# A hybrid decoder layer on one core: weight blocks with their k-tiles woven column by column

## What is computed

```python
xn = rmsnorm(x, mix_norm_g)
p = xn @ w_in                       # one projection, 1024 -> 10,256 columns
ya, yb, yc, yd = mlstm(...), short_conv_mixer(...), mamba2_mixer(...), stick_breaking_attention(...)
lifted = einsum('bsie,ied->bsid', stack([ya, yb, yc, yd]), w_lift)
merged = einsum('bsid,bsid->bsd', sigmoid(gates), lifted)
x = x + merged @ w_out
x = x + conv_glu_mlp(rmsnorm(x, ffn_norm_g), w_up, ffn_conv_w, ffn_conv_b, w_down)   # D_FF = 2816
return rmsnorm(x, final_norm_g)
```

## Time and profile before

| | |
|---|---|
| median of the runs | 1038.17 us (2 runs, 1037.79 to 1038.56) |
| the profiled execution | 1038.42 us |
| its span, first to last instruction | 1036.7 us |
| busy PE | 1019.0 us, 98% |
| busy PEld | 837.8 us, 81% |
| busy DVE | 593.2 us, 57% |
| busy ACT | 424.3 us, 41% |
| DMA | 108.24 MB, mean 104 GB/s |
| mean granted TensorE clock | 0.992 of full speed (2.4 GHz) |

### The profile page before, as it was taken

How to read it: one execution, slowest core, us unless ns; L and a number is a source line. 1 busy time by engine, 2 the same in 40 slices (tenths; PEclk the granted TensorE clock), 3 DMA queues, 4 the chain that set the end, 5 groups by cost and what they waited for, 6 DMA issues and landing times.

```text
span 1036.7 us, 12635 instructions
## 1 busy us (share of the span) xinstructions
PE 1019.0 (98%) x4724; PEld 837.8 (81%) x4724; DVE 593.2 (57%) x764; ACT 424.3 (41%) x515; POOL 67.6 (7%) x74
## 2 busy tenths in 40 slices
PE   8999999999999999999999999989999999999996
PEld 7897888887777887777888888868888888888886
DVE  6835754656676566556364456687656666543323
ACT  5514445644435322444432333544444344332331
POOL 5610000000000000000000000320000000000002
PEclk9999999999999999999999999989999999999998
DMA  6332222223222333343252222513233222253312
GB/s 238 114 113 70 82 84 82 77 93 105 89 85 82 120 122 124 132 132 103 81 183 87 97 88 97 181 61 119 85 100 101 100 86 88 68 176 94 102 56 81
DMA packets 32024, 108.24 MB, mean 104 GB/s; under 512 B 3684, under 2 KB 5860, under 8 KB 31600
## 3 DMA queue, kind: packets, MB, share of 16 engines
q1 hardware_dynamic: 29520, 93.86, 27.1%
q0 software_dynamic: 2320, 13.69, 4.0%
q10 hardware_dynamic: 144, 0.14, 0.1%
HBM read 103.42 MB, written 4.25 MB: 104 GB/s over the span
## 4 chain that ended last, share of the span: by engine, by line
PE 93%; DVE 4%; ACT 2%; issue 1%; DMA 1%; DVEq 0%; SPq 0%; ACTq 0%
PE gb L413 81%; PE gb L446 4%; DVE w_lo L985 1%; PE xb L596 1%; PE gb L524 1%; PE xb L556 1%; PE xb L549 1%; PE xb L536 1%; PE xb L413 1%; ACT w_hi L701 1%; PE xb L513 1%; DMA raw<-w_stream 1%; DVE y_lo L993 1%; PE gb L464 1%; PE xb L584 0%
## 5 line engine op out<-in xcount | busy, mean ns | idle before, releaser
L985 DVE TENSOR_TENSOR w_lo<-raw,w_hi 128x1024 fp32r<-128x1024 f32 (+2 forms) x181 | 218.1, 1206 | 342.8 <-ACT w_hi L701 342.4
L701 ACT ACTIVATE w_hi<-raw 128x1024 fp32r<-128x1024 f32 (+2 forms) x181 | 183.8, 1017 | 413.5 <-PE gb L413 380.8
L413 PE MATMUL gb<-xn_hi,w_hi 128*128 128x512 f32 x720 | 285.0, 396 | 0.0
L413 PE MATMUL gb<-xn_hi,w_lo 128*128 128x512 f32 x720 | 281.1, 390 | 0.0
L413 PE MATMUL gb<-xn_lo,w_hi 128*128 128x512 f32 x720 | 281.0, 390 | 0.0
L413 PE MATMUL gb<-y_hi,w_hi 128*128 128x512 f32 x400 | 159.1, 398 | 6.0 <-DVE y_lo L993 4.2
L413 PEld LDWEIGHTS gb<-xn_hi,w_hi 128*128 128x128 f32 x720 | 135.8, 189 | 29.7 <-issue 1.0
L413 PEld LDWEIGHTS gb<-xn_lo,w_hi 128*128 128x128 f32 x720 | 135.8, 189 | 29.0 <-issue 1.4
L413 PEld LDWEIGHTS gb<-xn_hi,w_lo 128*128 128x128 f32 x720 | 135.6, 188 | 28.6
L413 PE MATMUL gb<-y_lo,w_hi 128*128 128x512 f32 x400 | 156.6, 391 | 0.0
L413 PE MATMUL gb<-y_hi,w_lo 128*128 128x512 f32 x400 | 156.4, 391 | 0.0
(11 more groups left out here) (231 smaller groups left out, 1018.4 us busy)
## 6 DMA issues: line engine op xcount, KB each, us to landing
raw<-w_stream SPq DMA_DIRECT2D x149, 512.0 KB, 3.3
raw<-w_down SPq DMA_DIRECT2D x16, 384.0 KB, 3.0
abc<-scr_a POOLq DMA_DIRECT2D x8, 640.0 KB, 4.1
raw<-w_down SPq DMA_DIRECT2D x16, 320.0 KB, 2.8
x_in<-xT SPq DMA_DIRECT2D x8, 256.0 KB, 6.5
x<-xT POOLq DMA_DIRECT2D x1, 2048.0 KB, 8.5
scr_x<-x POOLq DMA_DIRECT2D x1, 2048.0 KB, 7.4
x<-scr_x POOLq DMA_DIRECT2D x1, 2048.0 KB, 8.4
```

The costliest lines, as they stand in the source:

```text
L413: ins = pe.matmul(out, w[:, r, lo:hi], rhs(k)[x], start=(first and n == 0 and q == 0), stop=(last_ and n == len(ks) - 1 and q == 2))
L701: act.activation(w_hi[:, r, 0:n], raw[:, r, 0:n], ACT.Copy).then_inc(S["hi_ready"], 1)
L985: dve.tensor_tensor(w_lo[:, r, 0:n], raw[:, r, 0:n], w_hi[:, r, 0:n].bitcast(F32), ALU.subtract)\
```

## The change

The host weaves the k-tiles of a block column by column: column c of k-tile n now lies at c * 8 + n, so one k-tile's columns are 8 fp32 elements, 32 bytes, apart. In the down-projection the blocks have 6 or 5 k-tiles, and the step is 24 or 20 bytes. In a lift block the two outputs' four k-tiles each are woven as eight. On the chip only the weight operand of `gemm` and of the small block changes: it reads with that step instead of contiguously. The blocks with tokens on the partitions keep `slabs`. DMAs, splits, waits and the order of all instructions stay the same.

```diff
@@ -61,6 +61,7 @@
 DOWN_K0 = [0, 6, 12, 17]
 N_UNITS = U_DOWN + 4 * KD
 RING = 4
+LANES = 8
 
 GL = {U_GL_D: 0, U_GL_A: 1, U_GL_B: 0, U_GL_C: 1}
 
@@ -405,12 +406,16 @@
 
     @block.tensor
     def _(pe):
-        def gemm(out, r, c0, rhs, ks, kk0=0, kstep=1, first=True, last_=True):
+        def ktile(w, r, kk, lanes=LANES, n=P):
+
+            c0 = kk // lanes * lanes * P + kk % lanes
+            return w[:, r, c0:c0 + lanes * (n - 1) + 1:lanes]
+
+        def gemm(out, r, kk, rhs, ks, first=True, last_=True, lanes=LANES):
 
             for n, k in enumerate(ks):
-                lo, hi = c0 + n * P, c0 + n * P + P
                 for q, (w, x) in enumerate(((w_hi, 0), (w_hi, 1), (w_lo, 0))):
-                    ins = pe.matmul(out, w[:, r, lo:hi], rhs(k)[x], start=(first and n == 0 and q == 0),
+                    ins = pe.matmul(out, ktile(w, r, kk + n, lanes), rhs(k)[x], start=(first and n == 0 and q == 0),
                                     stop=(last_ and n == len(ks) - 1 and q == 2))
             return ins
 
@@ -457,11 +462,11 @@
                 def yk(k):
                     return y_hi[s][:, k, :], y_lo[s][:, k, :]
                 for q in range(2):
-                    ins = gemm(gb(o + q)[:, :], u % RING, q * T, yk, range(4))
+                    ins = gemm(gb(o + q)[:, :], u % RING, 4 * q, yk, range(4))
             elif u == U_SMALL:
                 for k in range(KD):
                     for q, (w, x) in enumerate(((w_hi, 0), (w_hi, 1), (w_lo, 0))):
-                        ins = pe.matmul(gb(o)[0:96, :], w[:, u % RING, P * k:P * k + 96], xn(k)[x],
+                        ins = pe.matmul(gb(o)[0:96, :], ktile(w, u % RING, k, n=96), xn(k)[x],
                                         start=(k == 0 and q == 0), stop=(k == KD - 1 and q == 2))
             else:
                 ins = gemm(gb(o)[:, :], u % RING, 0, xg if u < U_DV else xn, range(KD))
@@ -477,7 +482,7 @@
             for u in (0, 1):
                 if k == 0:
                     pe.wait_ge(S["lo_ready"], u + 1)
-                ins = gemm(GB[u][:, :], u, k * P, xg, [k], first=(k == 0), last_=(k == KD - 1))
+                ins = gemm(GB[u][:, :], u, k, xg, [k], first=(k == 0), last_=(k == KD - 1))
         ins.then_inc(S["unit_done"], 2)
 
         for u in range(U_OUT):
@@ -608,7 +613,7 @@
             for k in range(KD):
                 if u == U_OUT:
                     pe.wait_ge(S["merged_ready"], k + 1)
-                ins = gemm(gb(first_tile[u])[:, :], u % RING, k * P, mg, [k], first=(k == 0), last_=(k == KD - 1))
+                ins = gemm(gb(first_tile[u])[:, :], u % RING, k, mg, [k], first=(k == 0), last_=(k == KD - 1))
             ins.then_inc(S["unit_done"], 1)
 
 
@@ -648,7 +653,7 @@
                 if t == 0:
                     pe.wait_ge(S["f_lo"], DOWN_K0[q] + DOWN_K[q])
                 gemm(GB[DOWN_BANK[t]][:, :], (U_DOWN + q) % RING, 0, hk, range(DOWN_K0[q], DOWN_K0[q] + DOWN_K[q]),
-                     first=(q == 0), last_=(q == 3)).then_inc(S["unit_done"], 1)
+                     first=(q == 0), last_=(q == 3), lanes=DOWN_K[q]).then_inc(S["unit_done"], 1)
         with pe.Fori(0, KD // 2 - 1) as i:
             for t in range(2):
                 down(i, t)
@@ -669,7 +674,8 @@
                 if e == 0 and q == 0:
                     pe.wait_ge(S["psum_read_dve"], DOWN_READ + KD - 2)
                 ins = gemm(O_LAST[e][:, 0:TH], (U_DOWN + q) % RING, 0, hk_half,
-                           range(DOWN_K0[q], DOWN_K0[q] + DOWN_K[q]), first=(q == 0), last_=(q == 3))
+                           range(DOWN_K0[q], DOWN_K0[q] + DOWN_K[q]), first=(q == 0), last_=(q == 3),
+                           lanes=DOWN_K[q])
                 if e == 1 and q == 0:
                     last_sum(0)
             ins.then_inc(S["o_last"], 1)
...
@@ -1412,9 +1418,15 @@
     (aq, ak, av, ao, ai, af, bb, bc, bx, cz, cx, cdt, sq, sk, sv, gt) = [w_in[:, c[n]:c[n + 1]] for n in range(16)]
     stream = np.zeros((N_STREAM, P, 1024), np.float32)
 
+    def lanes(w, n=LANES):
+
+        k, c = w.shape
+        w = w.reshape(k // (P * n), n, P, c).transpose(2, 0, 3, 1)
+        return np.ascontiguousarray(w).reshape(P, -1)
+
     def put(u, w, width=P):
         for n in range(w.shape[1] // width):
-            stream[u + n] = slabs(w[:, n * width:(n + 1) * width])
+            stream[u + n] = lanes(w[:, n * width:(n + 1) * width])
 
     def put_tokens(u, w):
         for n in range(2):
@@ -1424,30 +1436,31 @@
     put(U_DQ, sq); put(U_DK, sk); put_tokens(U_DV, sv)
     small = np.zeros((D, P), np.float32)
     small[:, 0:4], small[:, 32:36], small[:, 64:72] = ai, af, cdt
-    stream[U_SMALL] = slabs(small)
+    stream[U_SMALL] = lanes(small)
     put(U_AQ, aq); put(U_AK, ak); put_tokens(U_AV, av); put(U_AO, ao)
     put(U_Z, cz); put(U_XBC, cx)
     for n in range(4):
         for q, w in enumerate((bc, bx, bb)):
-            stream[U_B + 3 * n + q] = slabs(w[:, n * P:n * P + P])
+            stream[U_B + 3 * n + q] = lanes(w[:, n * P:n * P + P])
     lift = f["w_lift"][0]
     for u0, b in ((U_GL_D, 3), (U_GL_A, 0), (U_GL_B, 1), (U_GL_C, 2)):
         for t in range(4):
             for q in range(2):
                 d0 = P * (2 * t + q)
-                stream[u0 + 3 * t + q] = slabs(gt[:, D * b + d0:D * b + d0 + P])
-                stream[u0 + 3 * t + 2, :, 512 * q:512 * q + 512] = slabs(lift[b][:, d0:d0 + P])
+                stream[u0 + 3 * t + q] = lanes(gt[:, D * b + d0:D * b + d0 + P])
+            both = [lift[b][:, P * n:P * n + P] for n in (2 * t, 2 * t + 1)]
+            stream[u0 + 3 * t + 2] = lanes(np.concatenate(both))
     put(U_OUT, f["w_out"][0])
     up = f["w_up"][0]
     for t in range(NFF):
         for q in range(2):
-            stream[U_UP + 2 * t + q] = slabs(up[:, FF * q + P * t:FF * q + P * t + P])
+            stream[U_UP + 2 * t + q] = lanes(up[:, FF * q + P * t:FF * q + P * t + P])
     down = np.zeros((4 * KD, P, 6 * P), np.float32)
     wd = f["w_down"][0]
     for t in range(KD):
         for q in range(4):
             k0, n = DOWN_K0[q], DOWN_K[q]
-            down[4 * t + q, :, 0:n * P] = slabs(wd[k0 * P:(k0 + n) * P, t * P:t * P + P])
+            down[4 * t + q, :, 0:n * P] = lanes(wd[k0 * P:(k0 + n) * P, t * P:t * P + P], n)
 
     def cols(v):
```

More of the change, by code:

```diff
@@ L624, in _ @@
                         pe.matmul(X[0][:, :], ones[:], f_ac[:], start=True, stop=True).then_inc(S["n2_sum"], 1)
-                ins = gemm(gb(first_tile[u])[:, :], u % RING, k * P, x1g, [k], first=(k == 0), last_=(k == KD - 1))
+                ins = gemm(gb(first_tile[u])[:, :], u % RING, k, x1g, [k], first=(k == 0), last_=(k == KD - 1))
             ins.then_inc(S["unit_done"], 1)
@@ L635, in _ @@
                         pe.wait_ge(S["n2_ready"], k + 1)
-                    ins = gemm(GB[(TILES0 + BANK0 + q) % 4][:, :], (U_UP + q) % RING, k * P, mg, [k], first=(k == 0),
+                    ins = gemm(GB[(TILES0 + BANK0 + q) % 4][:, :], (U_UP + q) % RING, k, mg, [k], first=(k == 0),
                                last_=(k == KD - 1))
```

## The result

The woven kernel takes 1113.84 us (2 runs, 1112.41 to 1115.26) against 1038.17 us: 7.3% slower, ratio 1.0729 with a 95% interval of 1.0667 to 1.079. I had forecast 1054 us with a range up to 1077. The span of the profiled execution grew from 1036.7 to 1110.7 us, by 74.0 us.

A forecast was written before the change was run, and what follows sets the result against it. It took TensorE's matmuls, their number times a pace, to bound the kernel. 1038.4 us plus 0, 12.9 (last tile) and 3.1 (uncovered loads) gave 1054.4, stated as 1054, range 1036 to 1077 us.

The forecast's parts named there:

- The frame: Whole kernel: time is a number of matmuls times a pace; layout, split and DMA cost nothing, token blocks stay unchanged.
- Step one: 3822 matmuls of 512 columns in `gemm`: loads at 218 ns stay under the 227 ns pace, cost 0.
- the doubled reading: Strided weight loads of 128 columns read for 213 ns, twice as long, at 1.67 ns per new 16-byte piece.
- a fixed swap: Every `gemm` matmul: 13.3 ns on top of columns / 2.4, the same at 512 and 256 columns.
- A cover of 115 ns: 512-column matmuls: pace of 227 ns against 112 for loads alone hides longer loads; 9 ns left after the change.
- The prediction's last sentence: Signs of being wrong: step's price over 1.73 ns per column, or starts over 227 ns apart with short loads.
- Step two: Last tile, 132 matmuls of 256 columns: 218 ns replaces 120, 98 ns each, 12.9 us.
- Step three: Loads no fast matmul covers, after waits and the mixers' fp32 matmuls: 29 x 107 ns, 3.1 us.
- The free step: Rival, 31%: strided loads lose nothing and stay at 188 ns; time 1038 us, at most 1040.
- the heavy bound: Rival, 17%: each load element waits for the store, TensorE paces at 325 or 432 ns; 1448 or 1872 us.
- The load just exceeds its cover: Rival, 9%: the 13.3 ns swap follows the load, pace 232 ns in both streams; 1075 us.
- its threshold of 1.73: Load price in ns per column, (227 - 5) / 128, deciding that rival; only 0.06 above the proven rate.

The follow-up runs named there:

- first streams: Only fp32r matmuls with weight loads, no decoder layer, twelve load steps by matmul width; 512 columns: 226.7 ns at 4 bytes, 243.8 at 32.
- second streams: Matmul-and-load-only kernels, real moving operand against one repeated column; 512 columns, 32-byte load: 244.8 against 237.8 ns; contiguous load: 226.7 against 215.8.
- the streams: Kernels without the decoder layer: rows of 33 fp32r matmuls with loads of one step, nothing beside them; only start-to-start distance counts.
- the timed kernels: Against the kernel before: only the last projection woven, 1055.84 us (18.5 us more); only that projection's last tile woven, 1051.3 us (14.3 us more).

## Why the prediction was wrong

**The frame held.** The kernel is a number of matmuls times a pace; no layout, split or DMA cost anything, and the token blocks kept their loads. The size is explained by the paces: 3360 matmuls of 512 columns at 32 bytes, 17.1 ns each by the first streams (243.8 less 226.7), 57.5 us by that for 57.4 measured; and the last projection, 462 x 11 ns and 132 x 107.5 ns, 19.3 us for 18.5 measured. The second streams have 244.8 ns, which would give 60.8 us, so the streams price the kernel to some 3 us.

**Step one failed.** It read "218 is under 227 ... Cost 0" and cost about 62 us, 57.4 in the blocks before the last projection and 4 to 5 in seven tiles of it (18.5 less 14.3 by the timed kernels, 5.0 by the traces). Two terms in it were wrong, and they are different in kind:

- *The price of the load.* I took the doubled reading, 218 ns, from the fastest rate of new pieces that the contiguous moving operand shows. At 64 bytes the load alone takes 217 ns and at 20 and 24 about 222, so a doubling is near the truth for these steps; at this kernel's 32 bytes it is 238 ns, above the cover of 227 by itself. The inference from one operand's rate to the other's had no basis: a moving operand at 32 bytes takes a new piece every 0.84 ns where the load needs 1.86 (237.8 / 128). I read a rate that was merely used as if it were the limit.
- *The cover.* I took 226.7 ns as the matmul's own property, 213.3 and a fixed swap, "there is no loss to relieve". The clash streams show 215.8 ns without the moving operand's reads. The reads of the load and those of the matmul beside it get in each other's way (in which part of the chip isn't shown), and a load whose reads are scattered does so more: 6.4 ns per matmul at 8 bytes, with the load fully covered. A cover of 115 ns says when the load ends, not what it costs the work that covers it.

Of the 18.1 ns in the second streams (244.8 less 226.7), 11.1 are there by the load alone (237.8 less 226.7) and 7.0 by the clash on top (244.8 less 237.8). The prediction's last sentence names just these two as the signs of being wrong, a price over 1.73 ns per column and a moving stream slowed by a strided load, yet the second had no term in the sum and no chance of its own.

**Step two held, a little low.** 12.9 us foretold for the last tile, 14.3 measured: 226 ns from start to start where I had 218. In the streams the load alone takes 221 to 222 ns at these steps, and 227 to 228 under the real moving operand of 256 columns.

**Step three held for each start and was cancelled in the sum.** I had taken 3.1 us for 29 uncovered starts of 107 ns. The traces show 13 first matmuls of a block, right behind a mixer's matmuls, whose distance to the next start was 313 to 337 ns before and is 443 to 472 ns now, some 130 ns more each and 1.7 us together. One of them, before and after:

```profile
202.91 0.48 PE L413 MATMUL gb<-xn_hi,w_hi 128*128 128x512 f32 x1
203.23 0.39 PE L413 MATMUL gb<-xn_lo,w_hi 128*128 128x512 f32 x1
```

```profile
210.80 0.61 PE L418 MATMUL gb<-xn_hi,w_hi 128*128 128x512 f32 x1
211.24 0.41 PE L418 MATMUL gb<-xn_lo,w_hi 128*128 128x512 f32 x1
```

Against it, PE waited less for the splits. Its wait for `y_lo` fell from 4.2 to 2.8 us:

```profile
PE gb L418 <- DVE y_lo L999: 2.8, 1, 2.8
```

And in the profiled executions fewer of the 3360 matmuls ran at the half granted clock, the 1.2 GHz level, 8 and not 20; there a matmul takes 427 ns in both kernels. So they grew by 55.4 us, less than the 58 that 17.4 ns each would give. Whether the weaving caused the difference in clock isn't shown.

**The rivals.** The free step falls with the loads of 331 ns, and the heavy bound with a pace of 245 and not 325. "The load just exceeds its cover", 9% and 1075 us, was nearest, for its first part: reckoned as its threshold of 1.73 was, the price per column is 1.82 ns, (237.8 - 5) / 128. (Its pace of 232 should read 213 + 5 + 13.3 = 231.3, which makes its sum some 3 us less.) Its mechanism, a swap of 13.3 ns that follows the load, is not what happens: with one repeated column the 32-byte stream has 237.8 ns at 256 and at 512 columns alike, the same as the load alone. My range ended where that rival's sum did, and the 9 ns of margin in step one rested on a rate that nothing had tested. By its number the result falls into the 17% beyond 1077 us, but not by that case's mechanism.

**Two hits in a line.** The Trainium skill (SBUF — State Buffer, section Specifications (TRN2)) asks for two hits in a 16-byte line. For the load's own time the streams agree in the main: 118 ns with two hits, 175 with one and a third, 217 to 268 with one, against 112. The rule doesn't speak of the slowed matmul, and for the moving operand it doesn't hold here: at 8 bytes, two hits in a line, 512 columns take 453 ns and not 227.

## What to carry to other kernels

Keep both operands of a matmul contiguous in SBUF; for fp32r even a step of two elements costs 6 ns per 512-column matmul on the weight side (nothing at 384 columns or 256) and doubles the time on the moving side. Work that is covered is free only if it shares nothing with its cover: before costing it at nothing, measure the covering operation with the covered one changed alone. And where a trace shows a rate in use, that rate is a lower bound of what the unit can do, and for that unit alone, so a margin of a few per cent built on it should carry little of the chance.

## What the runs showed of the hardware

- With contiguous loads of 128 fp32r columns beside them, 512-column matmuls start 226.7 ns apart, and 215.8 with a moving operand of one repeated column. Nearly all of the gap to 213.3 ns goes with the moving operand's reads; what part of it the load causes isn't shown.
- The price of a load alone isn't monotonic in its step: 216.9 ns at 64 bytes, 268.4 at 48, 237.8 at 32.
- A load whose reads take longer than 213 ns doesn't slow with the array's clock: at 16 bytes and 128 columns the starts were 233 ns apart at the full granted clock and 233 at half (the 1.2 GHz level). Faster ones do: streams of 64 columns went from 112 to 214 ns with contiguous loads and from 118 to 213 at 8 bytes.
- At that half level 512-column matmuls started 427 ns apart, 512 / 1.2, with contiguous loads in the kernel before and with loads of every step from 8 to 128 bytes in the streams. Neither the swap nor the clash shows there.
- Not all of the clash is understood: with 8-byte loads a 256-column matmul keeps its 120 ns and a 384-column one its 173.5; at 448 it costs 0.6 ns, and only at 512 do 6.6 ns appear. Why it needs a long matmul wasn't settled.
